# Output projection with the tokens stationary and its weights resident, in a one-core encoder layer

## The reference

```python
mix = (g_a * y_a + g_b * y_b + g_c * y_c) @ w["w_o"]          # w_o: 1024 x 1024
x = layer_norm(ALPHA * x + mix, w["ln1_g"], w["ln1_b"])
f, conv_new = conv_ffn(x, conv_hist, w["w_up"], w["conv_w"], w["conv_b"], w["w_down"])
x = layer_norm(ALPHA * x + f, w["ln2_g"], w["ln2_b"])
# conv_ffn: u = x @ w_up (2 x 2816 columns), causal conv of width 3, gelu(gate) * val, @ w_down
```

## Time and profile before

| | |
|---|---|
| median of 3 runs | 1978.9 us (1977.29 to 1979.46) |
| profiled execution, its own time | 1974.96 us |
| its span | 1973.0 us |
| PE busy | 1871.6 us, 95% |
| DVE, ACT, POOL busy | 978.7, 748.1, 231.2 us |
| mean granted clock | 0.97 of full speed |

### The profile page before, as it was taken

The page is one execution under the profiler, slowest core; times in us unless marked ns, Lnnn a source line. Parts: engine busy times, 40 slices in busy tenths (PEclk is TensorE's granted clock), DMA queues, the critical chain, the costliest instruction groups (busy, mean ns, idle before and its releaser), DMA issues. The chain is left out here.

```text
span 1973.0 us, 32267 instructions
## 1 busy us (share of the span) xinstructions
PE 1871.6 (95%) x12315; PEld 1790.2 (91%) x12315; DVE 978.7 (50%) x1362; ACT 748.1 (38%) x1362; POOL 231.2 (12%) x333
## 2 busy tenths in 40 slices
PE   7999999999999899998999984999999999999997
PEld 7999799998998589997998884899999999999996
DVE  3100134344111555555665353876777777555465
ACT  3111223242211244445333365544545445443332
POOL 0000000001000310000000000333333332001010
PEclk9999999998999899997999996999999999999998
DMA  5111112122311221111443541222222222683753
GB/s 151 43 53 43 33 54 77 51 75 51 105 44 52 87 66 44 40 44 49 137 142 110 149 139 49 65 88 65 86 76 67 94 65 77 220 269 126 241 167 114
DMA packets 196072, 182.71 MB, mean 93 GB/s; under 512 B 20605, under 2 KB 165326, under 8 KB 195997
## 3 DMA queue, kind: packets, MB, share of 16 engines
q1 hardware_dynamic: 194140, 175.68, 29.1%
q0 software_dynamic: 1856, 5.99, 0.9%
HBM read 146.20 MB, written 35.53 MB: 92 GB/s over the span
## 5 line engine op out<-in xcount | busy, mean ns | idle before, releaser
L899 PE MATMUL banks<-act_hi,w_hi 128*128 128x352 f32 (+2 forms) x1264 | 423.4, 335 | 4.0 <-DVE w_lo L2102 2.3
L900 PE MATMUL banks<-act_lo,w_hi 128*128 128x352 f32 (+2 forms) x1264 | 416.9, 330 | 0.0
L901 PE MATMUL banks<-act_hi,w_lo 128*128 128x352 f32 (+2 forms) x1264 | 416.4, 329 | 0.0
L1291 PE MATMUL banks<-xs_hi,a_hi 128*128 128x256 f32 (+1 forms) x1232 | 355.9, 289 | 11.1 <-DVE xs_lo L2242 7.1
L1291 PE MATMUL banks<-xs_lo,a_hi 128*128 128x256 f32 (+1 forms) x1232 | 355.0, 288 | 0.0
L1291 PE MATMUL banks<-xs_hi,a_lo 128*128 128x256 f32 (+1 forms) x1232 | 354.6, 288 | 0.0
L1894 DVE TENSOR_TENSOR w_lo<-w_raw,w_hi 128x1024 fp32r<-128x1024 f32 x70 | 85.7, 1225 | 408.7 <-ACT w_hi L1390 408.6
L899 PEld LDWEIGHTS banks<-act_hi,w_hi 128*128 128x128 f32 x1264 | 240.1, 190 | 19.3 <-issue 10.8
L1291 PEld LDWEIGHTS banks<-xs_hi,a_hi 128*128 128x128 f32 x1232 | 236.2, 192 | 12.7 <-DVE xs_lo L2242 7.7
L900 PEld LDWEIGHTS banks<-act_lo,w_hi 128*128 128x128 f32 x1264 | 240.3, 190 | 2.7
L901 PEld LDWEIGHTS banks<-act_hi,w_lo 128*128 128x128 f32 x1264 | 240.2, 190 | 2.8
(11 more groups left out here) (286 smaller groups left out, 3085.2 us busy)
## 6 DMA issues: line engine op xcount, KB each, us to landing
w_raw<-in_w_down SPq DMA_DIRECT2D x132, 256.0 KB, 3.2
w_raw<-in_w_in SPq DMA_DIRECT2D x100, 256.0 KB, 3.3
gate_in<-gates_scratch SPq DMA_DIRECT2D x24, 529.0 KB, 3.6
h_keep<-conv SPq DMA_DIRECT2D x22, 530.0 KB, 2.8
raw_b<-in_w_up SPq DMA_DIRECT2D x44, 256.0 KB, 3.7
w_raw<-in_w_up SPq DMA_DIRECT2D x44, 256.0 KB, 3.8
h_raw<-h_keep SPq DMA_DIRECT2D x22, 384.0 KB, 5.2
w_raw<-in_w_o SPq DMA_DIRECT2D x32, 256.0 KB, 3.3
```

The source lines that it names most:

```text
L899: pe.matmul(out, hi, b_hi, start=start, stop=False)
L900: pe.matmul(out, hi, b_lo, start=False, stop=False)
L901: return pe.matmul(out, lo, b_hi, start=False, stop=stop)
L1291: last = pe.matmul(out, a[j][:, k, :], x[s][j][:, k, :], start=fresh and k == 0 and n_ == 0, stop=k == 3 and n_ == 2, skip_group_check=True)
```

## The change

w_o is computed the other way round. The stationary operand is now a block of 128 tokens of the merged activations, the moving operand 512 columns of a weight row block. `wo_rows(k)` loads row block k (128 x 1024), `wo_split(k)` splits it into `wo`, which keeps all eight blocks, high and low, in the region of `z`. `wo_tile(p)` makes one token tile, 8 x 6 matmuls of 512 columns, nine tiles in the order 0 to 5, 8, 6, 7 (`TILES`; tile 8 takes the last 128 columns, which overlap tile 7). Its result has token rows already: `acc`, `wo_out` and `r1` are gone, and VectorE reads the banks directly. The layer norm applies gain and bias in rows (`gain`, `shift`, with `ln_g`, `ln_b` broadcast to all partitions), and `x1_out` is one copy of 1024 columns. The operands of x for the first token half are laid into the region of `act_hi` and `act_lo`, over columns that w_o has finished; the second half's go to `z`'s region. Even slices of w_up now come to `w_raw`, odd ones to free blocks of the same region. In slice 0 all seven products of the first half run before those of the second.

```diff
-T_FFN = 86
+T_FFN = 78
...
+    wo = at("wo", [P, KD, 2, D], F32R, offset=Z_AT)
+    wo_hi, wo_lo = wo[:, :, 0], wo[:, :, 1]
...
-        def wo_tile(k):
-            cols((T_WO + k) // 2, k % 2, w_o, k % KD * P)
+        def wo_rows(k):
+            load((T_WO + k) // 2, k % 2, [(flat(k % 2, i, 512), w_o[:, k, 512 * i:512 * i + 512]) for i in range(2)])
...
+        for p in range(2):
+            load_rows(p)
+        sp.dma_start(ln_g[:, :], I["ln1_g"].to_broadcast([P, D])).then_inc(q.ln_consts, 16)
+        sp.dma_start(ln_b[:, :], I["ln1_b"].to_broadcast([P, D])).then_inc(q.ln_consts, 16)
+        for k in range(6, KD):
+            wo_rows(k)
...
+        sp.wait_ge(q.w_split_lo, T_FFN)
         raw_pair(0, 0)
...
+        for p in range(9):
+            if p + 2 < 9:
+                sp.wait_ge(q.x1_turned, p + 1)
+                load_rows(p + 2)
+            c, w = keep_cols(TILES[p])
+            sp.wait_ge(q.x1_acc_done, p + 1)
+            if TILES[p] >= NT - 1:
...
-        for t in range(9):
-            if t + 4 < 9:
-                sp.wait_ge(q.x1_turned, t + 1)
...
+            if p == 8:
+                sp.wait_ge(q.a_lo_done, a_count(0, 4))
+                sp.wait_ge(q.a_summed, 4)
+                sp.wait_ge(q.combined[0], 3)
                 raw_pair(1, 1)
+            sp.dma_start(x1_keep[:, :, c:c + w], x1_cols(c, w)).then_inc(q.kept, 16)
...
-                pool.wait_ge(q.out_mm, 24)
+                pool.wait_ge(q.out_mm, 9)
...
+        def wo_tile(p):
+            c, b = wo_at(TILES[p]), mix_bank(p)
+            if p == 0:
+                pe.wait_ge(q.k_out_ready, 1)
+            elif p == 1:
+                pe.wait_ge(q.part_done, 72)
+            else:
+                pe.wait_ge(q.r_done, p - 1)
             for k in range(KD):
-                last = pe.transpose(pair8(6)[:, k, 0:w], rows1[t % 4][0:w, k // 4, k % 4 * P:(k % 4 + 1) * P], ident[0:w, 0:w])
+                if p == 0:
+                    pe.wait_ge(q.mix_ready, k + 1)
+                    pe.wait_ge(q.w_split_lo, T_WO + k + 1)
+                for n_, (x, w) in enumerate(((act_hi, wo_hi), (act_hi, wo_lo), (act_lo, wo_hi))):
+                    for half in range(2):
+                        last = pe.matmul(bank(b + half), x[:, k, c:c + P], w[:, k, 512 * half:512 * half + 512],
+                                         start=k == 0 and n_ == 0, stop=k == KD - 1 and n_ == 2, skip_group_check=True)
+            last.then_inc(q.out_mm, 1)
...
+        def x1(p):
+            pe.wait_ge(q.shifted, p + 1)
+            pe.wait_ge(q.x1_acc_done, p)
+            for k in range(KD):
+                last = pe.transpose(pair8(6)[:, k, :], rows[p % 2][:, k * P:(k + 1) * P], ident[:, :])
             last.then_inc(q.x1_turned, 1)
 
-        ln_at = {8: [(r1, 0)], 10: [(r1, 1)], 11: [(x1, 0)], 12: [(r1, 2)], 13: [(x1, 1)], 14: [(r1, 3)], 15: [(x1, 2)], 17: [(x1, 3)]}
-        for k in range(2 * KD):
-            pe.wait_ge(q.w_split_lo, T_WO + k + 1)
-            for gi in ((0,), (1, 2))[k // KD]:
-                c, w = WG[gi]
-                y = k if gi == 0 else 2 * k - KD + gi - 1
-                if y >= 4:
-                    pe.wait_ge(q.out_free, y - 3)
-                else:
-                    pe.wait_ge(q.part_done, 69 + y)
-                dense(bank(y % 4)[:, 0:w], wo_hi[k // KD][k % 2], wo_lo[k // KD][k % 2], c, w,
-                      q.mix_ready if y == 0 else None).then_inc(q.out_mm, 1)
-                for step, t in ln_at.get(y, ()):
-                    step(t)
+        wo_tile(0)
+        for p in range(1, 9):
+            wo_tile(p)
+            x1(p - 1)
...
-        pe.wait_ge(q.out_free, 21)
-        block_product(0, 0, 0, 0, True)
-        r1(4)
-        block_product(0, 0, 0, 1, True)
-        r1(5)
-        block_product(0, 0, 0, 2, True)
-        r1(6)
-        block_product(0, 0, 0, 3, True)
-        x1(4)
-        r1(7)
-        block_product(0, 0, 0, 4, True)
-        x1(5)
-        r1(8)
+        for j in range(5):
+            block_product(0, 0, 0, j, True)
+        x1(8)
         block_product(0, 0, 0, 5, True)
-        for t in (6, 7, 8):
-            x1(t)
-        for j in range(6):
+        block_product(0, 0, 0, 6, True)
+        for j in range(NA):
             block_product(0, 0, 1, j, True)
...
             if k < 4:
                 split_hi((T_MERGE + k + 8) // 2, k % 2, used=(q.y_mm, 36 + 6 * (k + 1)))
+        act.wait_ge(q.y_mm, 60)
         wo_split(0)
+        wo_split(1)
+        act.wait_ge(q.y_mm, 66)
+        wo_split(2)
+        wo_split(3)
         mix_out(6)
         mix_out(7)
         act.wait_ge(q.y_mm, 72)
         act.wait_ge(q.part_done, 72)
-        wo_split(1)
...
-        def x1_out(t):
-            c, w = tok(t)
-            act.wait_ge(q.x1_turned, t + 1)
-            for k in range(KD):
-                last = act.activation(acc[:, k, c:c + w], pair8(6)[:, k, 0:w], ACT.Identity, scale=prm[:, PLG + k:PLG + k + 1],
-                                      bias=prm[:, PLB + k:PLB + k + 1])
...
+        def x1_out(p):
+            c, w = tok(TILES[p])
+            act.wait_ge(q.x1_turned, p + 1)
+            act.activation(x1_cols(c, w), pair8(6)[:, :, P - w:P], ACT.Copy).then_inc(q.x1_acc_done, 1)
...
             merge_tile(1, k, False)
             if k < 4:
                 split_lo((T_MERGE + k + 8) // 2, k % 2)
-        wo_split(0)
+            if k == 4:
+                wo_split(0)
+                wo_split(1)
         mix_lo(6)
+        wo_split(2)
         mix_lo(7)
-        for k in range(1, KD + 2):
+        for k in range(3, KD):
...
+        def ln1_stats(p):
+            buf, b = rows[p % 2], mix_bank(p)
+            dve.wait_ge(q.out_mm, p + 1)
+            dve.wait_ge(x_landed[p % 2], 16 * (p // 2 + 2))
+            dve.scalar_tensor_tensor(buf[:, :], buf[:, :], ALPHA, psum[:, b:b + 2, :].rearrange("p b c -> p (b c)"),
+                                     ALU.mult, ALU.add).then_inc(q.r_done, 1)
+            dve.wait_ge(q.r_done, p + 1)
+            stats(p, p % 2, P, [buf[:, 512 * s:512 * s + 512] for s in range(2)])
+        def ln1_gain(p):
+            gain(p, p % 2, P, rows[p % 2][:, :], rows[p % 2][:, :], 32)
+        def ln1_shift(p):
+            inverse_sd(p, p % 2, P)
+            shift(p, p % 2, P, rows[p % 2][:, :])
+        def ln1(p):
+            ln1_stats(p)
+            ln1_gain(p)
+            ln1_shift(p)
...
+        for p in range(8):
+            ln1(p)
+            if p == 4:
+                x_sum(0, 1)
+                x_low(0, 0)
+                a_low(0, 0, 0)
+                a_low(0, 0, 1, a_sum_first)
+            if p == 5:
+                x_sum(0, 2)
+                x_low(0, 1)
+                x_sum(0, 6)
+                x_low(0, 2)
+                a_low(0, 0, 3)
+            if p == 6:
+                x_low(0, 6)
+                x_sum(0, 4)
+                x_low(0, 3)
+            if p == 7:
+                x_low(0, 4)
+        ln1_stats(8)
+        a_low(0, 0, 2, a_sum_first)
+        ln1_gain(8)
+        ln1_shift(8)
+        a_low(0, 0, 4, a_sum_first)
+        x_low(0, 5)
+        a_low(0, 0, 5, a_sum_first)
+        dve.wait_ge(q.kept, 16 * 8)
...
+        combine(0, 0, 0, 0)
+        combine(0, 0, 0, 1)
         a_low(0, 0, 6)
-        for t in (7, 8):
-            ln1(t)
-            ln1_inverse(t)
-        dve.wait_ge(q.cleared, 3)
         x_sum(1, 1)
         x_low(1, 0)
+        combine(0, 0, 0, 2)
         x_sum(1, 2)
         x_low(1, 1)
         x_sum(1, 6)
         x_low(1, 2)
         x_low(1, 3)
         x_sum(1, 4)
+        x_low(1, 4)
+        a_low(1, 1, 0)
         x_low(1, 5)
-        x_low(1, 4)
+        a_low(1, 1, 1)
         x_low(1, 6)
+        a_low(1, 1, 2)
         dve.wait_ge(q.kept, KEPT)
         for par in range(2):
```

More of the change, by code:

```diff
@@ L41 @@
 ORDER = (0, 1, 2, 3, 5, 4, 6)
[L42 removed]
+FIRST_ORDER = (0, 1, 3, 2, 4, 5, 6)
+TILES = (0, 1, 2, 3, 4, 5, 8, 6, 7)
 H = 4
@@ L220, in program @@
     o_hi = at("o_hi", [P, 12, TT], F32R, offset=B_AT)
-    acc = at("acc", [P, KD, TF], F32, offset=B_AT)
+    x1f = [at(f"x1f{i}", [P, KD, (512, TF - 512)[i]], F32, offset=B_AT + 512 * KD * 4 * i) for i in range(2)]
     ring = Arena(nc, R_AT, RING_BYTES)
@@ L330, in program @@
     ln_rs = [n.take(f"ln_rs{i}", [P, 1], F32) for i in range(2)]
-    ln_nm = [n.take(f"ln_nm{i}", [P, 1], F32) for i in range(2)]
     ROWS_AT = n.at
@@ new lines, in program @@
+    PLACE_HI = ((0, 0), (1, 0), (2, 0), (0, 2), (2, 2), (0, 3), (3, 0))
+    PLACE_LO = ((0, 1), (1, 1), (2, 1), (1, 2), (3, 2), (1, 3), (3, 1))
+    f = Arena(nc, Z_AT, Z_BYTES)
+    xs_hi, xs_lo, xs_sum = ([[block_of(t, *place) for place in places]] for t, places in
+                            ((x_free_r, PLACE_HI), (x_free_r, PLACE_LO), (x_free, PLACE_LO)))
+    second = [(f.take(f"xs_hi{j}", [P, 4, HALF[1]], F32R), f.at, f.take(f"xs_lo{j}", [P, 4, HALF[1]], F32R)) for j in range(NA)]
+    xs_hi.append([x[0][:, :, :] for x in second])
```

(32 more changed lines are left out.)

399 lines of the change are left out of this document (138 added, 261 removed).

## The result

The changed kernel has a median of 1945.3 us (four runs, 1942.1 to 1950.8) beside 1978.1 us for the kernel before; ratio 0.9837, 95% interval 0.9809 to 0.9865. Five more runs of it, beside other runs of before, had a ratio of 0.9849 (0.9827 to 0.9871), which is 30 us; there the medians, 1948.9 and 1975.4, lie 26.6 us apart. The prediction was 1951, with 1940 to 1965 as its range.

A forecast was written before the change was run, and what follows sets the result against it. It took slice 0 to be bound by a relay between engines, not by TensorE. Slice 0 ending at 1223.5 instead of 1252.6, less 1.1 for the rest, saves 28 us: 1978.9 - 28 = 1951, range 1940 to 1965.

The forecast's parts named there:

- Step 1: End of the branch merge: two early splits of w_o delay the last merge tile, 2 us lost.
- Step 2: Tile 0 of w_o: bound by the supply of w_o through two landing buffers, ending at 1095 instead of 1080.2.
- Rival A: Tile 0 of w_o: supply hidden, blocks 6 and 7 land with the rows, 15 us less, 1936; chance 0.12.
- Step 3: Eight more w_o tiles at 11.1 us plus transposes, layer norm covered; w_o ends at 1189.4, 12 us later than before.
- rival D: w_o's 432 matmuls: a new stationary load each, not overlapped, costs 188 ns apiece, 81 us, giving 2032; chance 0.05.
- Step 4: Slice 0: bound by VectorE, 34 us instead of 74.9, from 28 of work, 4 of waits and 2 at the end.
- Rival B: Slice 0 stays a relay, with waits repeating at the lower clock: tail 46 us, 12 more, 1963; chance 0.20.
- C: Slice 0 and tile 0 both go long: tail 54 us, tile 0 ending at 1099, total 1975; chance 0.03.
- Step 5: The rest: slice 1 starts with weight parts queued behind slice 0's work, about 1 us.

The follow-up runs named there:

- The second run: Changed kernel with VectorE splitting blocks 0 and 1 of w_o behind the last merge tile again, not ahead of it; 1951.3 us, ratio to the kernel before 0.9889.
- the two places: Changed kernel with two more landing places: blocks 4 and 5 of w_o land where the LayerNorm rows lie later; 1934.9 us, ratio to the kernel before 0.9795.
- operands behind w_o: Changed kernel with the first slice's operands formed from x1 only after the last w_o tile; 1959.1 us, ratio to the kernel before 0.9923.

## Why the prediction was right, and where it was not

- **Step 1** said 2 us of wait for `part` and had 1.5. The second run shows that the early splits pay for it.
- **Step 2** had the mechanism and nearly the size: first tile's end at 38.8, measured 37.4. Its two parts were tested apart: the burst of rows ahead of block 6 is worth 4.8 us, and with two more buffers 10.5 us of it fall away. The wait before block 6 was 5.6 us, not 7: block 6 landed 30.7 us after the gate load, not 31.9, and TensorE came to it 0.6 us later. The clock's loss was near 1.4 us (60 products in 15.39, 0.257 each, at 0.233 else), where 2 stood. Rival A (supply hidden, 1936) is what the two places make of the kernel: 1935.
- **Step 3** held: 95.20 us for 384 products and seven sets of transposes (5.6), 0.233 us a product, no wait, clock 1.00. A tile takes 12.0 us, not 11.9. PEld is busy 77.91 us beside it. By the rule of the Trainium skill (TensorE: Matmul & The Clock Gate, Part 3) that a stationary load overlaps matmuls in flight only when its row group differs, each product would pay both. The trace does not agree, now with the tokens stationary too, and rival D is out.
- **Step 4** said 34 us, with 28 of work on VectorE and waits mainly for `xs_lo`. It took 34.1, but two sizes in it were off and met. VectorE was busy 30.55 us and idle for only 3.5. What the sum did not have is GpSimd: two weight parts took 1.67 us beside it where 0.64 to 0.69 is usual, and one shift 2.12 where 1.28 is, 2.8 us in all. Of TensorE's 8.4 us of waits only 2.7 are for `xs_lo`; 2.2 are for a copy that stands on ScalarE behind splits of x and of a weight, which had waited for VectorE's fourth sum; 1.7 are for the last additions, behind a weight part. Rival B's relay is not there, nor C's long tail. Slice 0 is 40.9 us shorter than before (74.94, 34.09). The run "operands behind w_o" shows 14.3 of them; for the rest the 26.0 us of waits for the add and `x1_out` have about the size, but no run puts them back, so that part is argued from the rows.
- **Step 5** named the wrong cause, and its size came out by luck. It took 1.1 us for slice 1's late weight parts and small things; from the end of slice 0 to the end of the span it is 720.4 us before and 721.2 in the changed kernel, 0.8 lost. But the changed kernel waits nowhere in slice 1, where the kernel before still waited 1.5 and 0.7 us, so 2 were gained. Against them stands a cost that the prediction did not have: with x's operands in `act`'s region the 256-column products take some 2 ns longer, 22 slices of 84, 3 us over w_up. The two nearly cancel.
- The sum, 28 us, is 29.0 from the common zero. The median fell by 33 because the two profiled executions lie 3.1 us to either side of their medians, and the start of the program varies by several us by itself. So most of the 6 us between 1951 and the 1945 measured are spread that the working does not treat; with the other runs of before the medians are 26.6 apart.

## What to carry to other kernels

When a resident operand is filled through few landing buffers, price the chain land, cast, subtract, reissue, and look for memory that is free only then: the places of two rows wanted later gave 10 us. Keep loads that nobody needs yet behind those that the chain waits for. A stall in a transition between two stages moves on when its last link is shortened; read the next stage's waits before counting it, and measure from a common event, since totals hid an effect of 5 us.
